# Two heads per transpose: splitting the rotated queries and keys of NSA and differential attention behind TensorE instead of before it

## What is computed

```python
def partial_rope(x, positions):          # rotates the first 16 of 64 columns of a head
    ...
def nsa_mixer(x, w_in, ...):
    q, kc, vc, ks, vs, kw, vw, gates = split(x @ w_in)
    q_rot = partial_rope(q * Dh ** -0.5)
    s = einsum('bqghd,bqgnkd->bqghnk', q_rot, k_sel);   o_slc = softmax(s) @ v_sel
    s = einsum('bqghd,bkgd->bqghk', q_rot, k_win);      o_win = softmax(s) @ v_win
    return (g0 * o_cmp + g1 * o_slc + g2 * o_win) @ w_out
def diff_mixer(x, k1, k2, v, w_q, ...):  # k1, k2 are rotated too
    a = softmax(q1 @ k1) - lam * softmax(q2 @ k2)
    return rms_norm(a @ v) @ w_out
for layer in range(2):
    x = post_norm(x, 0.5 * swiglu(x)); x = post_norm(x, mixer(x)); x = post_norm(x, 0.5 * swiglu(x))
    if layer == 0: k1, k2, v = shared_kv(x)
```

## Time and profile before

| | |
|---|---|
| median of 3 runs | 1014.42 us |
| profiled execution | 1013.32 us, span 1011.4 us |
| TensorE busy | 998.2 us, 99% of the span |
| DVE, ACT, POOL busy | 664.6, 469.5, 103.7 us |
| chain that ended last | 94% on PE, 2% on DVE, 2% on ACT |
| granted TensorE clock | 0.999 of full speed |

### The profile page before, as it was taken

How to read it: one execution, slowest core, us unless ns; L and a number is a source line. 1 busy time by engine, 2 the same in 40 slices (tenths; PEclk the granted TensorE clock), 3 DMA queues, 4 the chain that set the end, 5 groups by cost and what they waited for, 6 DMA issues and landing times.

```text
span 1011.4 us, 13543 instructions
## 1 busy us (share of the span) xinstructions
PE 998.2 (99%) x5374; PEld 850.5 (84%) x5374; DVE 664.6 (66%) x653; ACT 469.5 (46%) x632; POOL 103.7 (10%) x141
## 2 busy tenths in 40 slices
PE   9999999999999999999999999999998999999997
PEld 7888888888888888888888888888887788888885
DVE  5876763765856667674575567774598877677544
ACT  7544433444864544343443444333468655434430
POOL 0020000222920100000022000000033110000000
PEclk9999999999999999999999999999999999999999
DMA  9866554560223755554447664654459366555431
GB/s 333 295 213 223 199 209 172 195 221 1 87 95 96 249 183 173 212 196 167 167 167 234 217 215 166 207 208 166 167 173 160 126 208 210 165 180 215 146 123 42
DMA packets 80060, 181.58 MB, mean 180 GB/s; under 512 B 3392, under 2 KB 9680, under 8 KB 80016
## 3 DMA queue, kind: packets, MB, share of 16 engines
q1 hardware_dynamic: 73312, 170.21, 48.4%
q0 software_dynamic: 6704, 10.76, 4.4%
HBM read 177.81 MB, written 1.05 MB: 177 GB/s over the span
## 4 chain that ended last, share of the span: by engine, by line
PE 94%; DVE 2%; ACT 2%; DMA 0%; issue 0%; POOL 0%; POOLq 0%; SPq 0%; DVEq 0%; ACTq 0%
PE acc L1479 15%; PE acc L1481 15%; PE acc L1480 15%; PE acc L1579 13%; PE aux L1579 7%; PE acc L1581 7%; PE trb L1579 6%; PE trb L1529 4%; PE aux L1581 4%; PE trb L1581 3%; PE acc L1737 1%; PE acc L1600 1%; PE acc L1597 1%; PE acc L1601 1%; PE aux L1781 1%; ACT norm_gb L782 1%
## 5 line engine op out<-in xcount | busy, mean ns | idle before, releaser
L968 DVE TENSOR_TENSOR w_lo<-raw,w_hi 128x2048 fp32r<-128x2048 f32 x148 | 336.6, 2283 | 174.0 <-ACT w_hi L674 173.9
L674 ACT ACTIVATE w_hi<-raw 128x2048 fp32r<-128x2048 f32 x148 | 280.3, 1902 | 152.4 <-PE acc L1481 124.3
L1579 PE MATMUL acc<-xt,w_hi 128*128 128x512 f32 x576 | 205.0, 395 | 0.0
L1581 PE MATMUL acc<-xt,w_lo 128*128 128x256 f32 x576 | 161.6, 280 | 0.0
L1479 PE MATMUL acc<-w_hi,ht_hi 128*128 128x512 f32 x352 | 137.0, 389 | 0.0
L1481 PE MATMUL acc<-w_hi,ht_lo 128*128 128x512 f32 x352 | 136.8, 389 | 0.0
L1480 PE MATMUL acc<-w_lo,ht_hi 128*128 128x512 f32 x352 | 136.8, 389 | 0.0
L1579 PEld LDWEIGHTS acc<-xt,w_hi 128*128 128x128 f32 x576 | 108.0, 187 | 25.4
L1479 PE MATMUL acc<-w_hi,xt 128*128 128x512 f32 (+1 forms) x320 | 127.3, 398 | 0.2 <-DVE xt L983 0.2
L1481 PE MATMUL acc<-w_hi,xt 128*128 128x512 f32 (+1 forms) x320 | 123.5, 386 | 0.0
L1480 PE MATMUL acc<-w_lo,xt 128*128 128x512 f32 (+1 forms) x320 | 123.4, 385 | 0.0
(11 more groups left out here) (233 smaller groups left out, 1306.8 us busy)
## 6 DMA issues: line engine op xcount, KB each, us to landing
raw<-ffn_gate_up SPq DMA_DIRECT2D x84, 1024.0 KB, 5.2
raw<-ffn_w_down SPq DMA_DIRECT2D x44, 1024.0 KB, 4.9
raw<-w_kv SPq DMA_DIRECT2D x8, 1024.0 KB, 6.2
raw<-w_in SPq DMA_DIRECT2D x6, 1024.0 KB, 5.2
raw<-ffn_gate_up SPq DMA_DIRECT2D x16, 256.0 KB, 6.1
raw<-w_out_a SPq DMA_DIRECT2D x4, 1024.0 KB, 6.0
raw<-w_q SPq DMA_DIRECT2D x4, 1024.0 KB, 5.1
raw<-w_out_b SPq DMA_DIRECT2D x4, 1024.0 KB, 5.5
```

The costliest lines, as they stand in the source:

```text
L674: act.activation(w_hi[:, slot, 0:k * c], raw[:, slot, 0:k * c], ACT.Copy).then_inc(hi_ready, 1)
L968: dve.tensor_tensor(w_lo[:, slot, 0:k * c], raw[:, slot, 0:k * c], w_hi[:, slot, 0:k * c].bitcast(F32), ALU.subtract).then_inc(lo_ready, 1)
L1579: pe.matmul(bank.rearrange("p (a s) -> p a s", a=2), hi[:, k, cols], xt[:, :, kt, :], start=(kt == 0), stop=False)
L1581: ins = pe.matmul(bank[:, 0:SEQ], lo[:, k, cols], xt_hi[:, kt, :], start=False, stop=(kt == KT - 1))
```

## The change

The rotated rows are no longer split before they are turned. TensorE turns 128 columns of plain fp32, that is two heads at once: the even head comes to lie in partitions 0 to 63 of `trb`, the odd one in 64 to 127, and one bank holds 8 heads. Then ACT writes the hi part of each half to the same partitions (two instructions on 64 partitions), and DVE subtracts and writes the lo part to the other half of the partitions (two more). An odd head thus has lo above hi; since keys are treated alike or are used with both orders, the scores are the same. A bank of `trb` is given free by DVE and no longer by the one engine that copied it.

The number of turns of four transposes falls from 8 to 4 each for NSA's queries, the differential keys and the differential queries, from 24 to 12 in all. NSA's tile 0 queries are turned between the last projection products and no longer behind the compressed scores; its tile 1 queries in steps 6 and 11 and no longer in 6, 9, 11 and 13; the late differential queries in steps 2 and 6, one turn each, and no longer in steps 0, 2 and 6, two each. The differential queries get a buffer of their own (`dq = y`), which takes one wait away.

```diff
-LATE_PARTS = {"nsa": {6: (0,), 9: (1,), 11: (2,), 13: (3,)}}
+LATE_PARTS = {"nsa": {6: (0,), 11: (1,)}}
-DIFF_EARLY = [("kr", tok, part) for tok in range(TOKS) for part in range(4)] + [("qr", 0, 0), ("qr", 0, 1)]
-DIFF_LATE = {0: ((("qr", 0, 2),), (("qr", 0, 3),)), 2: ((("qr", 1, 0),), (("qr", 1, 1),)),
-             6: ((("qr", 1, 2),), (("qr", 1, 3),))}
+DIFF_EARLY = [("kr", 0, 0), ("kr", 0, 1), ("kr", 1, 0), ("kr", 1, 1), ("qr", 0, 0), ("qr", 0, 1)]
+DIFF_LATE = {2: ("qr", 1, 0), 6: ("qr", 1, 1)}
...
+        def stacked(heads, part, tok):
+
+            at = [(slice(8 * part + r, 8 * part + 8, 2), slice(tok * P, (tok + 1) * P)) for r in range(2)]
+            top, low = slice(0, DH), slice(DH, P)
+            return [(top, heads[top, at[0][0], at[0][1]], heads[low, at[0][0], at[0][1]]),
+                    (low, heads[low, at[1][0], at[1][1]], heads[top, at[1][0], at[1][1]])]
...
+            def queries_high(tok, part):            # ACT; stacked_high is the same for keys and queries of diff
+
+                t = TURN_OF["qr", "nsa", tok, part]
+                act.wait_ge(tr_full, t + 1)
+                turned = trb[:, t % 2].rearrange("p (k c) -> p k c", c=P)
+                for at, hi, lo in stacked(nqs[:], part, tok):
+                    ins = act.activation(hi, turned[at], ACT.Copy)
+                ins.then_inc(tr_hi, 1)
...
             for i, sc, tr, pv in job_steps(NSA_JOBS):      # ACT
                 if tr:
                     copy_p("nsa", i - 2)
-                for part in LATE_PARTS["nsa"].get(i, ()):
-                    copy_heads(("qr", "nsa"), 1, part, nqs)
                 if sc:
                     exps("nsa", NSA_JOBS, i, 0)
+                for part in LATE_PARTS["nsa"].get(i, ()):
+                    queries_high(1, part)
-                if i == 3:
-                    split_beside(3)
...
             for i, sc, tr, pv in job_steps(DIFF_JOBS):     # ACT
-                for name, tok, part in DIFF_LATE.get(i, ((), ()))[0]:
-                    copy_keys_or_queries(name, tok, part)
                 if sc:
                     exps("diff", DIFF_JOBS, i, len(NSA_JOBS))
                 if tr:
                     copy_joined(i - 2)
+                if i in DIFF_LATE:
+                    stacked_high(*DIFF_LATE[i])
...
+            def queries_low(tok, part):             # DVE; stacked_low is the same for diff
+
+                t = TURN_OF["qr", "nsa", tok, part]
+                dve.wait_ge(tr_hi, SPLIT_OF["qr", "nsa", tok, part] + 1)
+                turned = trb[:, t % 2].rearrange("p (k c) -> p k c", c=P)
+                for at, hi, lo in stacked(nqs[:], part, tok):
+                    ins = dve.tensor_tensor(lo, turned[at], hi.bitcast(F32), ALU.subtract)
+                ins.then_inc(tr_free[t % 2], 1)
...
-                if i == 4:                                  # DVE, NSA steps
-                    split_beside(3)
+                for part in LATE_PARTS["nsa"].get(i, ()):
+                    queries_low(1, part)
...
-                for name, tok, part in DIFF_LATE.get(i, ((), ()))[1]:   # DVE, differential steps, behind join_maps
-                    copy_heads(name, tok, part)
-                if i == 5:
-                    split_beside(9)
+                if i in DIFF_LATE:
+                    stacked_low(*DIFF_LATE[i])
...
-                   3: lambda: (second_layer(), *(swap_halves(...)))},   # PE, NSA's last projection group
+                   3: second_layer},
+                  inner={..., 2: {2 + half: lambda half=half: turn_queries(0, half) for half in range(2)},
+                         3: {1 + m: lambda m=m: swap_halves(...) for m in range(2)}})
             compressed_scores(0)
-            for part in range(4):
-                turn_heads(("qr", "nsa"), 0, part, 2)
...
             run_units(1, n0, (0,), columns_unit, inner={0: {1: early[0], 3: early[1]}})   # PE, differential queries
-            run_units(1, n0, (1,), columns_unit, inner={0: {k: early[2 + k] for k in range(4)}})
+            run_units(1, n0, (1,), columns_unit, inner={0: {1: early[2], 3: early[3]}})
             query_piece(0)
-            early[6]()
-            early[7]()
+            early[4]()
             query_piece(1)
-            early[8]()
             query_piece(2)
-            early[9]()
+            early[5]()
             query_piece(3)
```

More of the change, by code:

```diff
@@ L158, in pair @@
         turn.extend([(*name, 0), (*name, 1)])
-    def four(*name):
-        turn.extend([(*name, part) for part in range(4)])
     for stage in STAGES:
@@ L168, in count_events @@
             pair("q", 0)
-            turn.extend([("kr", 0), ("kr", 1), ("ks", 0), ("ks", 1)])
-            four("qr", "nsa", 0)
+            turn.extend([("kr", 0), ("kr", 1)])
+            pair("qr", "nsa", 0)
+            turn.extend([("ks", 0), ("ks", 1)])
             for i, _, tr, pv in job_steps(NSA_JOBS):
@@ L185, in count_events @@
             for i, _, tr, pv in job_steps(DIFF_JOBS):
-                first, second = DIFF_LATE.get(i, ((), ()))
-                turn.extend([(name, "diff", tok, part) for name, tok, part in first])
                 if tr:
                     turn.append(("p", "diff", i - 2))
-                turn.extend([(name, "diff", tok, part) for name, tok, part in second])
+                if i in DIFF_LATE:
+                    name, tok, half = DIFF_LATE[i]
+                    turn.append((name, "diff", tok, half))
                 if i in TILE0_DONE["diff"]:
@@ L637, in swap_keys @@
                 for half in range(2):
-                    for part in (2 * half, 2 * half + 1):
-                        t = TURN_OF["kr", "diff", tok, part]
-                        pool.wait_ge(tr_free[t % 2], t // 2 + 1)
+                    t = TURN_OF["kr", "diff", tok, half]
+                    pool.wait_ge(tr_free[t % 2], t // 2 + 1)
                     at = slice(8 * half, 8 * half + 8), slice(tok * P, (tok + 1) * P)
@@ L869, in _ @@
             ins.then_inc(gate_exp, 1)
-            for part in range(4):
-                copy_heads(("qr", "nsa"), 0, part, nqs)
+            for j in range(2):
+                copy_turned(("ks", j), nks[:, 1, j].rearrange("p g (t c) -> p (g t) c", c=P))
             def compressed_exp(tok):
@@ L905, in _ @@
             n0 = UNIT_OF["diff_q"]
-            for k in range(4, 6):
-                split_beside(k)
             x_high("ffn2", 1)
@@ L1234, in _ @@
             ins.then_inc(cmp_ready, 1)
+            for part in range(2):
+                queries_low(0, part)
             dve.wait_ge(cmp_full, 1)
@@ L1246, in _ @@
             ins.then_inc(cmp_ready, 1)
-            split_beside(2)
             dve.wait_ge(gate_exp, 1)
@@ L1798, in turn_q, with turn_queries @@
                 turn_wide(("q", tok), nq[:, tok, :])
-            def turn_heads(name, tok, part, k):
-                pe.wait_ge(beside_ready, k + 1)
-                turn((*name, tok, part), [beside[k][:, 4 * part + j].rearrange("p s d -> p (s d)").bitcast(F32)
-                                          for j in range(4)])
+            def turn_queries(tok, half):
+                pe.wait_ge(rope_done, 3 + tok)
+                turn(("qr", "nsa", tok, half), [nq[:, tok, half * 512 + j * P:half * 512 + (j + 1) * P] for j in range(4)])
             def compressed_scores(tok, pairs=range(NSA_HEADS // 2)):
@@ L1919, in _, with diff_turn @@
             n0, e = UNIT_OF["diff_q"], FILL_OF["diff_q", 0, 0]
-            def diff_turn(name, tok, part):
-                k, at = (4 + tok, part) if name == "kr" else (6 + 2 * tok + part // 2, part % 2)
-                pe.wait_ge(beside_ready, k + 1)
-                turn((name, "diff", tok, part), [beside[k][:, 4 * at + j].rearrange("p s d -> p (s d)").bitcast(F32)
-                                                 for j in range(4)])
+            def diff_turn(name, tok, half):
+                pe.wait_ge(rope_done, 5 + tok if name == "kr" else 7 + 2 * tok + half)
+                src = {"kr": k_nat, "qr": dq}[name][:, tok, half * 512:(half + 1) * 512]
+                turn((name, "diff", tok, half), [src[:, j * P:(j + 1) * P] for j in range(4)])
             def query_piece(kt):
@@ L1993, in _ @@
                     tok, half = i // 4 > 0, int(i in (2, 8))
-                    for m in range(2):
-                        copied("qr", "diff", int(tok), 2 * half + m)
+                    copied("qr", "diff", int(tok), half)
                     for t in range(tok + 1):
```

116 lines of the change are left out of this document (55 added, 61 removed).

## The result

The changed kernel takes 1024.51 us, median of 5 runs (1022.39 to 1025.5), against 1014.72 us for the kernel before beside it (1013.09 to 1015.1): ratio 1.0089, 95% interval 1.0074 to 1.0104. It is 9.8 us slower by the medians; forecast were 1019.5 us, with a range of its own to 1021.5 and one for 8 in 10 to 1023. The sign was right, the size was not.

What follows compares the result with a forecast made beforehand. TensorE was taken as the bound around attention, but inside it the loop of scores, DVE maximum, ACT exponentials, turn and values. NSA +1.9 and differential +4.3 made +6.2 on 1013.3: 1019.5 us, range 1018 to 1021.5, 8 in 10 1013.5 to 1023.

Steps and rivals of the forecast that it cites:

- The low pair: DVE's two lo instructions for a bank, on 64 partitions each, behind ACT's hi pair: taken as 1.3 us.
- step 2: Differential attention: DVE stands 1.8 us for hi, then lo; TensorE's turn of joined maps comes at 779.5, +3.0 us.
- step 6: Differential attention: hi and lo run to 788.0 ahead of `diff_norm`, delaying it and the values of job 4, +4.3 us.
- NSA's step 6: Hi waits behind exponentials, lo ends at 262.4, `nsa_mix` queues behind; values of job 4 move to 265.8, +2.6 us.
- The three rivals on the cheap side: TensorE savings all pay, 1008.0 (10%); pairs half as long, 1015.3 (8%); one standing time covered, 1017 to 1018 (18%).
- TensorE's 5.3 us: Twelve of 24 turns go at 0.44 us each: 5.3 us saved if TensorE were the bound at each.
- The fourth, dearer pairs: Rival: pairs cost up to 2.4 us for lo, 1.1 more in three steps; 1023 to 1024 us, 7%.
- The fifth: Rival: NSA's early turns find rows not rotated and stop the projection; a few tenths lost, no chance of its own.
- differential stage, to the first scores: Start of differential attention: bank waits and DVE's queue, running to 765.4, cost +0.6 us despite 1.8 us less work.
- its steps, clock at full speed: Differential attention's steps behind the first scores: +3.7 us, within the stage's +4.3.
- 0.2 given back: NSA behind step 6: two turns fewer save 0.9 us, less 0.2 for step 11's bank being free late in step 13.
- afterwards TensorE is the bound, so nothing is given back: Differential attention behind the values of job 4: TensorE is the bound to the stage's end, so its +4.3 us stays.

Runs made afterwards that it cites:

- diff_only: Against the kernel before: differential attention as changed, NSA as before; 1023.23 us, ratio 1.0069.
- nsa_only: Against the kernel before: NSA attention as changed, differential attention as before; 1018.41 us, ratio 1.0024.
- high_first: Against the changed kernel: in the late steps of both attentions ACT takes the high pair ahead of the exponentials; 1019.55 us, ratio 1.0039.
- filled: Against the changed kernel: 25 useless matmuls added in TensorE's three long waits of differential attention; 1022.16 us, ratio 1.0053.
- order_e: Against the changed kernel: NSA as in high_first, late differential pairs on steps 0 and 5, low parts of output weights moved later; 1018.54 us, ratio 1.0041.
- before_again: The kernel before profiled once more, no edit; 1015.44 us in its one run.
- high_filled: Against high_first: 20 useless matmuls added in three TensorE waits of differential attention; 1018.58 us, ratio 1.0034.

## Why the prediction was right and wrong

*Right, by the rows.* The low pair stands behind ACT, DVE behind it, TensorE behind both. `nsa_mix` at 262.41 (262.4 forecast; that it agrees so closely is luck, since the pairs took 1.22 + 1.39 us and not 2.4, and the stage's first mark lies 0.29 us earlier in this execution than in that of before); DVE idle 1.84 us in step 2 (1.8), 1.58 in step 6 and 3.04 in NSA's step 6 (1 to 3 for both); scores 4 waiting 1.73; the fourth turn of keys waiting 1.40 (1.1) and the second turn of queries 1.23 (0.8). diff_only, nsa_only and high_first confirm the mechanism. The three rivals on the cheap side fell: a pair takes 1.18 to 1.22 and 1.39 us, not half, no wait was covered, and of TensorE's 5.3 us the two turns in NSA's late steps alone show as time won, the 0.9 that the forecast counted (point 3). The fourth, dearer pairs, comes nearest to the measured time with its 1023 to 1024, but not by its cause: 1.39 is not 2.4. The fifth did not occur: the early turns of NSA, at 236.05 and 237.18, wait for nothing.

*The low pair* was priced at 1.3 and took 1.39. The Trainium skill (VectorE: DVE Perf Modes, "Two Vector instructions with no wait between them") has the second instruction of such a pair, and what follows it, held until the one ahead has ended; the prediction had made 1.38 us of it, as an estimate. The trace agrees: the pair at 260.98 ends at 262.37 and the next instruction starts at 262.41, while behind the 128-partition pair at 754.72, which takes 1.29, the next starts at 755.93, 0.08 before its end.

*Wrong, the size.* From 1019.5 to 1024.5 are 5.0 us:

| term | forecast | measured | difference |
|---|---|---|---|
| where before stands (profiled run, median) | 1013.3 | 1014.7 | 1.4 |
| NSA | +1.9 | +2.45 | 0.55 |
| differential stage, to the first scores | +0.6 | +1.45 | 0.85 |
| its steps, clock at full speed | +3.7 | +3.55 | -0.15 |
| its steps, clock fallen | 0 | +2.4 | 2.4 |

1. **The sum lacked a term: the clock.** It treated TensorE's waits as lost time and its work behind them as equally fast. The kernel filled shows what the steps cost at full clock, 814.37 - 771.66 = 42.71 us from the first scores to the last turn against 803.95 - 764.79 = 39.16 before: +3.55, where 3.7 was forecast. It fits on the way, too: the turn of job 2's joined rows is +2.32 in filled (2.4 forecast). The changed kernel has 45.15. This is half of the whole miss, and the range had no room for it, since every row of before that I read in these stages has the clock at 1.00.
2. **The way to the first scores** was a queue on DVE, and I had summed it right in kind, but with 1.3 for a pair and no gaps: 6.7 us from 758.7 to 765.4. It is 770.10 - 762.94 = 7.16, begun 0.3 later. (The prediction speaks of seven pieces of weights between the five pairs; there are four, and its 6.7 us are worked out with the right ones.) The two differences, 0.46 and 0.3, make most of the 0.85. order_e shows that this queue was the bound: with two low parts of weights out of it the scores come 1.5 us earlier.
3. **NSA.** The values of job 4 came at 264.85 and not at 265.8: the gate's product took 0.18 us (L1314), and the forecast carried over the 1.15 that it had taken before. Why it was shorter is open; in step 11 it took 1.03 again. Counted from the stage's first mark the values are 1.97 us late and not 2.6. What that gave was lost at step 11's pair: the turn of step 13 waited 1.40 us for its bank where "0.2 given back" stood. 1.97 + 1.40 less the two turns' 0.9 make 2.47, and 2.45 were measured.
4. **The base.** The forecast named that the median might lie 1.1 above the profiled run, and kept the lower figure. before_again shows what was low about it: that profile had the short feed-forward stretch. The median is the better base.

The claim "afterwards TensorE is the bound, so nothing is given back" held at full clock: from the values of job 4 to the last turn it is 814.37 - 794.83 = 19.54 us in filled and 803.95 - 784.39 = 19.56 before. In the changed kernel it is 20.75, with the clock down.

## What to carry to other kernels

Here a wait of the busiest engine had two prices: its length, and what the clock took from the work behind it. The second could not be read from the profile of before, where the clock is 1.00. It shows in the windows of the first profile after, and filling the waits measures it. When one bank is emptied by two engines in a row, put the first engine's part ahead of work whose input comes later anyway: that one move won 4.4 to 5 thousandths here, part of it through the clock. Moving the second part back is not the same thing, since the bank stays held, and in NSA, where the next user of the bank is near, it cost more than it gave.

None of the versions beat the kernel before. Of those with both halves high_filled has the lowest ratio, 1.0034; the change in NSA alone has 1.0024 and 1.0020. What stays is about 0.5 us in NSA and 2 to 4 in differential attention. I put that down to steps where DVE and ACT are full anyway (in order_e TensorE waits 3.35 us for DVE), but no run tests it.

## What the hardware showed

- TensorE's clock went to the lower of its levels (granted 0.50; four score loads 0.97 us for 0.54, four value loads 0.93 to 0.98 for 0.52) in the second of two waits of 1.73 and 2.05 us, in differential attention in both profiles of the changed kernel; after NSA's wait of 1.8 us it fell in one profile and stayed in others with the same wait.
- Matmuls that nobody needs, in place of waits, kept the clock at 1.00 and made a kernel 3 us faster by the ratios, 2.4 us in the profile.
- One feed-forward stretch takes 158.3 or 160.05 us for the same instructions (391 or 399 ns a matmul of 512 columns), with the clock's row at 1.00 in both. Its cause is open.
- One instruction on 64 partitions with 512 elements takes 0.59 us on ACT and 0.69 on DVE, as on 128 partitions: what counts is the length of a row, not the partitions. Two in a row, on one half of the partitions and then the other, take 1.18 to 1.22 and 1.39 us, where two on all 128 took 1.09 and 1.29.
